# Turns and first scores of three attentions issued inside the projection panels ahead of them

## The reference, cut to what matters

```
(a_q, a_k, a_v, a_g, b_cq, b_ckv, b_kr, b_g, c_q, c_k, c_v, c_g) = split(h @ w_in)
o_a = dense attention, 8 query heads on 2 key heads, normalised and rotated q and k, times silu(a_g)
cq = rms_norm(b_cq);  q_nope, q_pe = split(cq @ w_uq);  q_pe is rotated
ckv = rms_norm(b_ckv); k_nope, vb = split(ckv @ w_ukv); k_pe = rotated b_kr
o_b = dense attention on [nope, pe], 4 heads, times silu(b_g)
o_c = neighbourhood attention with a bias table, 4 heads, times silu(c_g)
x + rms_norm(concat(o_a, o_b, o_c) @ w_out)
```

## Time and profile before

| what | us |
|---|---|
| median of 3 runs | 3577.71 (3576.12 to 3578.48) |
| the profiled execution's own time | 3576.41 |
| its span | 3574.4 |
| TensorE matmul busy | 3421.8 (96%) |
| VectorE busy | 1803.3 (50%) |
| ScalarE busy | 1099.3 (31%) |

### The profile page before, as it was taken

One profiled execution on the slowest core, in us unless ns is written; L12 is line 12 of the kernel. 1 busy time (PEld: TensorE's weight loads), 2 busy tenths in 40 slices (PEclk: granted clock), 3 DMA queues, 4 the chain that ended last, 5 costly groups with the idle time before them and its releaser, 6 DMA issues.

```text
span 3574.4 us, 49995 instructions
## 1 busy us (share of the span) xinstructions
PE 3421.8 (96%) x17285; PEld 2755.7 (77%) x17285; DVE 1803.3 (50%) x3264; ACT 1099.3 (31%) x1764; POOL 151.8 (4%) x218
## 2 busy tenths in 40 slices
PE   7999999999999999999997999999997999999997
PEld 6878878668788788786885888778786888778786
DVE  4555665544565557753456332625634332535643
ACT  3232243232232322522323222523323322433321
POOL 1101001000111010010010000000000000000000
PEclk9999999999999999999998999999998999999999
DMA  7636414215676363060364333033233333123242
GB/s 263 209 91 195 133 42 162 77 42 200 179 257 188 102 188 89 18 215 12 122 190 146 99 95 99 19 92 104 107 129 110 89 94 99 43 86 92 79 155 97
DMA packets 183840, 429.83 MB, mean 120 GB/s; under 512 B 18166, under 2 KB 25777, under 8 KB 177240
## 3 DMA queue, kind: packets, MB, share of 16 engines
q1 hardware_dynamic: 151144, 297.65, 26.1%
q0 software_dynamic: 28992, 104.43, 9.6%
q10 hardware_dynamic: 3504, 25.22, 1.8%
HBM read 406.15 MB, written 24.75 MB: 121 GB/s over the span
## 4 chain that ended last, share of the span: by engine, by line
PE 60%; DVE 4%; issue 1%; DMA 1%; ACT 1%; DVEq 0%; SPq 0%; ACTq 0%; POOLq 0%
PE bank L660 16%; PE bank L662 16%; PE bank L661 16%; PE bank L705 2%; PE bank L723 2%; PE bank L860 1%; PE bank L838 1%; PE bank L849 1%; PE bank L697 1%; PE bank L714 1%; PE bank L684 1%; DMA stage<-in_w_out 1%; PE bank L893 0%; DMA wmod<-in_w_mod 0%; PE bank L930 0%
## 5 line engine op out<-in xcount | busy, mean ns | idle before, releaser
L660 PE MATMUL bank<-wlo,act_hi 128*128 128x512 f32 (+1 forms) x3968 | 1552.3, 391 | 7.9 <-DVE zone L1483 4.6
L662 PE MATMUL bank<-whi,act_lo 128*128 128x512 f32 (+1 forms) x3968 | 1539.1, 388 | 0.0
L661 PE MATMUL bank<-whi,act_hi 128*128 128x512 f32 (+1 forms) x3968 | 1538.2, 388 | 0.0
L1436 DVE TENSOR_TENSOR wlo<-stage,whi 128x1024 fp32r<-128x1024 f32 (+1 forms) x496 | 598.3, 1210 | 794.1 <-ACT whi L1089 792.3
L1089 ACT ACTIVATE whi<-stage 128x1024 fp32r<-128x1024 f32 (+1 forms) x496 | 514.9, 1048 | 1458.0 <-PE bank L662 796.2
L660 PEld LDWEIGHTS bank<-wlo,act_hi 128*128 128x128 f32 x3968 | 747.1, 188 | 178.4 <-issue 21.2
L662 PEld LDWEIGHTS bank<-whi,act_lo 128*128 128x128 f32 x3968 | 746.4, 188 | 151.8
L661 PEld LDWEIGHTS bank<-whi,act_hi 128*128 128x128 f32 x3968 | 747.2, 188 | 145.9
L1451 DVE SCALAR_TENSOR_TENSOR macc<-wmod,csil,macc 128x512 f32<-128x512 f32 x360 | 270.0, 750 | 111.4 <-DMA wmod<-in_w_mod 82.3
L2275 POOL DMA_DIRECT2D wmod<-in_w_mod x192 | 136.6, 711 | 1736.9 <-DVE macc L1451 1720.9
L723 PE MATMUL bank<-zone 128*128 128x128 f32 x1024 | 134.7, 276 | 0.0
(11 more groups left out here) (236 smaller groups left out, 2308.3 us busy)
## 6 DMA issues: line engine op xcount, KB each, us to landing
stage<-in_w_in SPq DMA_DIRECT2D x352, 512.0 KB, 3.8
wmod<-in_w_mod POOLq DMA_DIRECT2D x192, 512.0 KB, 4.5
stage<-in_w_out SPq DMA_DIRECT2D x128, 512.0 KB, 4.1
out<-Y ACTq DMA_DIRECT2D x20, 1024.0 KB, 5.5
zone<-out SPq DMA_DIRECT2D x4, 4096.0 KB, 14.9
stage<-in_w_in SPq DMA_DIRECT2D x16, 320.0 KB, 3.8
Y<-in_x ACTq DMA_DIRECT2D x4, 1024.0 KB, 9.3
rpb_tiles<-rpb_pad POOLq DMA_DIRECT2D x16, 224.0 KB, 7.2
```

Of the source, the lines that this page charges most:

```text
L660: pe.matmul(out, hi_x, lo_w, start=(k == 0), stop=False)
L661: pe.matmul(out, hi_x, hi_w, start=False, stop=False)
L662: mm = pe.matmul(out, lo_x, hi_w, start=False, stop=(k == KC - 1))
L1436: dve.tensor_tensor(wlo[:, j % RH, :, 0:width], stage[:, j % RS, :, 0:width], whi[:, j % RH, :, 0:width].bitcast(F32), ALU.subtract).then_ ...
```

## The change

1. C: its 8 turn jobs are issued in panel 3, two after each of j = 0 to 3, into banks 4 and 5 (`job_bank`); after j = 6 its first two scores. VectorE takes the jobs at its own j = 2 to 5, takes the first two row maxima ahead of the gate, and ScalarE the first two exponentials ahead of the tanh. The tanh goes to another place (`tanh_c`).
2. A: in panel 8, after j = 4 the two key turns, after j = 5 the first query turn, after j = 6 two scores. The turn of head h + 1 moves from the first to the last unit of head h, into banks 2 and 3, and the next unit waits for its copy.
3. B: the turns of three cq chunks go behind j = 6 of panel 11 into banks 4 to 6 and are copied out by ScalarE after the tanh. The four v products alternate with the four q_pe turns, and head h waits for its own turn only.
4. P: in panel 6, the turns of 2 key and 2 query tiles after j = 0 to 3, two scores after j = 6. The later turns move to the last unit of a group of four, two groups ahead. Banks are dealt anew. The wait for all finishes at the end goes into panel 7, at its first use of banks 1 and 3.
5. `banks_free` before C, A and P goes; the units 2 and 3 wait for single banks, since turned probabilities now go to banks 0 and 1 (for P, bank 0).

The diff of TensorE's side, and of the others the lines that are spoken of (P's and C's parts on ScalarE and VectorE follow the same form):

```diff
-        PAIR_SCORE, PAIR_TURN, PAIR_OUT, PAIR_JOB = [bank[2:4], bank[4:6]], bank[6], [bank[7], bank[1]], bank[0]
+        PAIR_SCORE, PAIR_TURN, PAIR_OUT, PAIR_JOB = [bank[4:6], bank[6:8]], bank[0], [bank[1], bank[3]], bank[2]
         MSUM = bank[7]
         SIDE = bank[4:6]
+        EARLY = bank[4:7]
+        A_JOB = bank[2:4]
...
+        A_EARLY, P_EARLY, BEGUN = A_KV + 1, 4, 2
+        def job_bank(n):
+            if 1 <= n < 1 + 2 * C_H + A_EARLY:
+                return SIDE[n % 2]
+            if 1 <= n < 1 + 2 * C_H + A_KV + A_H:
+                return A_JOB[n % 2]
+            return JOB[n % 2]
...
-            def attention(blk, l, br, early=None):
+            def attention(blk, l, br, turned=None, more=None, opened=None):
                 n = 4 * br["heads"]
-                for i in range(n + 3):
-                    if early and i % 4 == 0 and i < n:
-                        early(i // 4)
+                for i in range(br["begun"], n + 3):
+                    if turned and i % 4 == 0 and i < n:
+                        turned(i // 4)
                     if i < n:
                         score(blk, l, br, i)
+                    if opened:
+                        opened(i)
+                    if more and i % 4 == 3 and i < n:
+                        more(i // 4)
...
-                with pe.Fori(1, 4) as p:
+                with pe.Fori(1, 3) as p:
                     panel(0, l, p, row=p - 1)
-                banks_free(l, 4)
-                pe.wait_ge(mod_ev.sem, mod_ev.at(0, l, 3))
-                for n, jb in enumerate(JOBS_C):
-                    job(0, l, BR_C["j0"] + n, jb)
-                pe.wait_ge(job_ev.sem, job_ev.at(0, l, BR_C["j0"] + 8))
-                attention(0, l, BR_C)
+                j0 = BR_C["j0"]
+                def begin_c(j):
+                    if j < 4:
+                        job(0, l, j0 + 2 * j, JOBS_C[2 * j])
+                        job(0, l, j0 + 2 * j + 1, JOBS_C[2 * j + 1])
+                    if j == 6:
+                        pe.wait_ge(job_ev.sem, job_ev.at(0, l, j0 + 8))
+                        apart(pe)
+                        for i in range(BEGUN):
+                            score(0, l, BR_C, i)
+                panel(0, l, 3, row=2, between=begin_c)
+                def opened_c(i):
+                    if i in (2, 3):
+                        pe.wait_ge(lin_free[i - 2].sem, lin_free[i - 2].at(0, l, 4))
+                    if i == 3:
+                        pe.wait_ge(mod_ev.sem, mod_ev.at(0, l, 3))
+                attention(0, l, BR_C, opened=opened_c)
...
-                panel(0, l, 8)
-                banks_free(l, 9)
-                pe.wait_ge(mod_ev.sem, mod_ev.at(0, l, 7))
-                pe.wait_ge(prep.sem, prep.at(0, l, A_READY + 1))
-                j0 = BR_A["j0"]
-                for n, jb in enumerate(JOBS_AK + JOBS_AQ[0:1]):
-                    job(0, l, j0 + n, jb)
-                def next_queries(h):
+                i0 = BR_A["j0"]
+                def begin_a(j):
+                    if j == 4:
+                        pe.wait_ge(prep.sem, prep.at(0, l, A_READY + 1))
+                        apart(pe)
+                        job(0, l, i0, JOBS_AK[0])
+                        job(0, l, i0 + 1, JOBS_AK[1])
+                    if j == 5:
+                        job(0, l, i0 + 2, JOBS_AQ[0])
+                    if j == 6:
+                        pe.wait_ge(job_ev.sem, job_ev.at(0, l, i0 + 3))
+                        apart(pe)
+                        for i in range(BEGUN):
+                            score(0, l, BR_A, i)
+                panel(0, l, 8, between=begin_a)
+                def opened_a(i):
+                    if i in (2, 3):
+                        pe.wait_ge(lin_free[i - 2].sem, lin_free[i - 2].at(0, l, 9))
+                    if i == 3:
+                        pe.wait_ge(mod_ev.sem, mod_ev.at(0, l, 7))
+                        for t in (2, 3):
+                            pe.wait_ge(lin_free[t].sem, lin_free[t].at(0, l, 9))
+                        apart(pe)
+                def turned_a(h):
+                    pe.wait_ge(job_ev.sem, job_ev.at(0, l, i0 + 3 + h))
+                    apart(pe)
+                def more_a(h):
                     if h + 1 < A_H:
-                        job(0, l, j0 + 3 + h, JOBS_AQ[h + 1])
-                    pe.wait_ge(job_ev.sem, job_ev.at(0, l, j0 + 3 + h))
-                attention(0, l, BR_A, next_queries)
+                        job(0, l, i0 + 3 + h, JOBS_AQ[h + 1])
+                attention(0, l, BR_A, turned_a, more_a, opened_a)
...
+                def begin_b(j):
+                    if j == 6:
+                        pe.wait_ge(prep.sem, prep.at(0, l, BTM_READY + 1))
+                        for r in range(3):
+                            apart(pe)
+                            for t in range(TT):
+                                mm = pe.transpose(EARLY[r][:, tok(t)], cq_b[:, t, tok(r)], ident[:, :])
+                            mm.then_inc(cq_turned.sem, 1)
+                panel(0, l, 11, row=8, between=begin_b)
...
+                pe.wait_ge(cq_out.sem, cq_out.at(0, l, 3))
+                apart(pe)
+                for jb in JOBS_B2[0:TT + 2 * B_H]:
                     job(0, l, n, jb)
                     n += 1
                 pe.wait_ge(prep.sem, prep.at(0, l, QPE_READY + 1))
-                for jb in JOBS_B3:
-                    job(0, l, n, jb)
-                    n += 1
-                pe.wait_ge(job_ev.sem, job_ev.at(0, l, n))
-                attention(0, l, BR_B)
+                apart(pe)
+                for h in range(B_H):
+                    job(0, l, n, JOBS_B2[TT + 2 * B_H + h])
+                    job(0, l, n + 1, JOBS_B3[h])
+                    n += 2
+                def turned_b(h):
+                    pe.wait_ge(job_ev.sem, job_ev.at(0, l, B_VQ + 2 * h + 2))
+                    apart(pe)
+                def opened_b(i):
+                    if i == 2:
+                        pe.wait_ge(job_ev.sem, job_ev.at(0, l, n))
+                        apart(pe)
+                attention(0, l, BR_B, turned_b, None, opened_b)
...
-                for n in range(J_KT, J_QT + 1):
-                    pair_job(l, n)
-                for i in range(PAIRS + 3):
+                for i in range(BEGUN, PAIRS + 3):
+                    hp = i // 4
                     if i % 4 == 0 and i < PAIRS:
-                        hp = i // 4
-                        if hp + 1 < S_H // 2:
-                            pair_job(l, J_QT + hp + 1)
                         pe.wait_ge(job_ev.sem, job_ev.at(1, l, J_QT + hp + 1))
+                        apart(pe)
                     if i < PAIRS:
                         pair_score(l, i)
+                    if i < 4:
+                        for t in ((0,), (1, 2, 3))[i - 2]:
+                            pe.wait_ge(lin_free[t].sem, lin_free[t].at(1, l, 7))
+                        apart(pe)
+                    if i % 4 == 3 and hp + 2 < S_H // 2:
+                        pair_job(l, J_QT + hp + 2)
                     if 2 <= i < PAIRS + 2:
                         pair_turn(l, i - 2)
                     if i >= 3:
                         pair_pv(l, i - 3)
-                pe.wait_ge(fin_done.sem, fin_done.at(1, l, PAIRS))
...
+                def begin_p(j):
+                    if j == 0:
+                        pe.wait_ge(prep.sem, prep.at(1, l, S_READY + 1))
+                        apart(pe)
+                    if j < P_EARLY:
+                        pair_job(l, J_KT + j)
+                    if j == 6:
+                        pe.wait_ge(job_ev.sem, job_ev.at(1, l, J_KT + P_EARLY))
+                        apart(pe)
+                        for i in range(BEGUN):
+                            pair_score(l, i)
+                panel(1, l, 6, between=begin_p)
                 swa(l)
                 apart(pe)
-                panel(1, l, 7, between=lambda j: rank_sums(l, j))
+                def last_pairs(t):
+                    if t in (1, 3):
+                        pe.wait_ge(fin_done.sem, fin_done.at(1, l, PAIRS - (t == 1)))
+                panel(1, l, 7, between=lambda j: rank_sums(l, j), opened=last_pairs)
...
                 if after:
                     for j in range(LEAD):
                         split_hi(blk, l, p + 1, j, next_width)
+                if begin:
+                    begin()
                 if row is not None:
                     mod_row_out(l, row)
                 if take:
...
-                in_panel(l, 3, take_tanh(), row=2)
+                in_panel(l, 3, take_tanh(tmp=tanh_c), row=2, begin=begun(BR_C, l))
...
+                act.wait_ge(lin_done.sem, lin_done.at(0, l, 12 * TT))
+                for r in range(3):
+                    act.wait_ge(cq_turned.sem, cq_turned.at(0, l, r + 1))
+                    act.activation(cqT[:, r, :], EARLY[r][:, :], ACT.Copy, scale=cols[:, B_QC + r:B_QC + r + 1])\
+                       .then_inc(cq_out.sem, 1)
```

(33 more changed lines are left out.)

132 lines of the change are left out of this document (72 added, 60 removed).

## The result

The changed kernel takes 3524.25 us (median of 4 runs, 3522.68 to 3526.52) against 3577.22 for the kernel before, run beside it; the ratio is 0.9849, 95% interval 0.9837 to 0.9862. That is 53.0 us less; a gain of 53.5 and a time of 3524.2 were forecast. The page's busy line answers to the earlier trace rows: TensorE lost 24 us of busy time (matmuls at the low clock count as longer) and the other 27 us are idle time.

A forecast was written before the change was run, and what follows sets the result against it. TensorE, with a matmul in flight for 96% of the span, was taken to bound the kernel; 13.0 + 10.5 + 3.9 + 3.2 + 2.8 + 17.9 + 2.2 = 53.5 us saved, 3577.7 - 53.5 = 3524.2, range 3512 to 3545.

The forecast's parts named there:

- C: Attention start at panel 3: 5.35 us inside plus 1.63 behind, 6.98 against 13.51; 13.0 us saved in two layers.
- A: Attention start at panel 8: 2.74 us inside, 5.8 in all against 11.55 and 10.54; 10.5 us saved.
- B: Attention start at panel 11: savings of 3.9 us at the start, 3.2 at values and q_pe turns, 2.8 for clock.
- P: Attention start at panel 6: 3.3 us inside, 3.6 behind, 17.9 saved; wait of 1.10 at the end hidden, 2.2 saved.
- B's clock: First score to unit 3's in B: full clock could give 5.5 us in both layers or nothing; half taken, 2.8.
- B's other two terms: Last panel matmul to first product in B, 3.9 us saved; values and q_pe turns, 1.6 a layer, 3.2 saved.
- score 2's price: Third score of C, behind the panel: 0.96 us with the change of operand type, 0.86 without.
- rival 2: Panels become bound by VectorE, `split_lo` and weight DMAs come late: 68 us lost against 53.5, 3592 us; chance 0.04.
- the head turns: Other six heads of A: each turn's copy takes about 1.45 us against 1.33 of cover; 0.12 each, 0.7 a layer.
- 1 (low clock comes back): Low clock returns at A, B and P, and A's head turns cost 0.5 each: gain 37, 3541 us; chance 0.19.
- Rival 3: Low clock vanishes everywhere and A's turns find their copy done: gain 59, 3519 us; chance 0.12.
- 4: First scores wait for their turns' copies after j = 6, so panels' idle only moves: gain some 20, 3558; chance 0.03.

The follow-up runs named there:

- late_c: The changed kernel with C's turns and first two scores behind panel 3 again, after all four gates: 3539.59 us.
- b_old: The changed kernel with B's cq turns behind panel 11 and v products ahead of the q_pe turns again; third bank, ScalarE copies, own-turn wait kept: 3523.47 us.
- late_p2: The changed kernel with P's four turns and first two scores behind panel 6 of the second block again: 3546.97 us.
- a_turn: The changed kernel with A's turn job of head h + 1 issued at the third unit of head h, save for the first head: 3522.75 us.

## Why the prediction was right, and where it was not

The time was forecast to 0.1 us (the gain to 0.5, as the kernel before ran 0.5 us faster beside it), but by misses that cancel, and that is luck: from the 53.5 of the sum, 2.4 more in B's clock, 1.1 in P, 0.35 in C and 1.7 elsewhere, against 6.3 at panels 10 and 11, 1.2 in A and 0.2 in B's other two terms, make the 51.3 of the two spans.

- **C** held step by step: 5.31 inside where 5.35 was forecast, 1.52 behind for 1.63. The 0.11 is what score 2's price held for a change of operand type: directly behind the panel's matmuls the first score takes 0.85 (212.98 to 213.83), so the 0.96 of the earlier trace rows came with the wait of 0.95 that stood ahead of that score, and not with the type. That the panel grows by just what is put in shows that VectorE never bound it; rival 2's place (`wlo` waits) stayed empty. late_c confirms the size (14.6, 1.0 of it clock).
- **A.** Inside 2.37 and 2.29 for 2.74. The failed term is the head turns: 0.29 each instead of 0.12. The score comes 1.96 us behind the start of the job, so 1.52 behind its end where I had 1.45 for the copy, against 1.33 of cover; and I had left out the 0.10 that TensorE loses as it starts again. The forecast's 2.63 to 2.8 between two scores with a head's turn job between them was 2.83 to 2.93.
- **B.** Both sizes were right and both reasons wrong. I gave the 1.6 a layer at the values to the alternation; b_old shows that the wait for one head instead of four earns it. The prediction's own working could have told: "three waits of 0.44 and one of 1.41 for three of 0.6" makes 0.9 and not 1.6, and by starts, less 0.44 for the turn, the waits of before are 0.60, 0.63 and 0.63, the same as in b_old, and 1.60 at the end. I gave the start to turns inside the panel; b_old does without them and keeps the gain, which leaves the third bank and ScalarE. Only a kernel that undoes one of several edits of a place could show this. The clock term came in full, 5.2 for the 5.5 it could be, where I took half; it went with the idle 1.41 ahead of the first score, with which the clock fell in 7 of 8 passes.
- **P.** 3.60 and 3.77 behind the panel for 3.6, 2.94 and 2.98 inside for 3.3, 1.30 for 1.10 at the end. late_p2 puts 19.8 us on the start, low clock included.
- **The failed step** is the sentence "No part of the chain outside these places changes: no DMA is added or moved". None is, in the program; but TensorE's code itself comes by DMA, and 405 instructions more ahead of panel 10 put one of its fetches into a stretch that is bound by transfers: 6.3 us lost at panels 10 and 11, of which 6.0 came back with the fetch moved. I had looked at how long the panels are and what waits in them, not at what the DMA queues of kind "instruction" do.
- **Rivals.** 1 (low clock comes back) held in half of B's starts, for 2 us each, not at A and P. In the profile of after that was no loss against before, whose clock fell there too. Rival 3's clock came, but not its other condition, that A's turns find their copy done. The Trainium skill's page "TensorE: Matmul & The Clock Gate", Part 1, says that the count of matmuls at the low clock varies from run to run. The trace agrees: at B's start in the first layer the four microseconds from 4 us behind the panel are at 0.54 in after and at 1.00 in a_turn, and TensorE's program there is the same. 4 had no part: no score inside a panel waits.

## What to carry to other kernels

Where an attention begins behind a projection, put its turns and first scores between the panel's matmuls: they cost what they cost elsewhere, and the wait for the gate, the copies and the first exponential goes, and with it the clock that those waits lose. After such an edit compare every stretch, also those that it does not touch: the count of instructions ahead of a transfer-bound stretch is a parameter of it, and a panel taken out of a loop changes it by some 400. And when several edits meet in one place, undo them one by one before one of them gets the credit.

## What the runs showed of the hardware

- With a fetch of code on a DMA queue (0.02 MB in 0.96 us) 9.7 to 10.7 us into panel 10, a 512 KB transfer comes 1.3 us later. From panel 10's first matmul to panel 11's last, B's turns taken off, it is 76.2 to 78.3 us in the 12 passes with no delay and 78.6 to 81.5 in the 14 with it. About half of the difference is low clock: with half of the time at 0.50 taken off (an estimate from the granted clocks), the two groups are 75.9 to 76.6 and 76.9 to 78.3.
- 96 semaphore increments among a panel's matmuls cost TensorE nothing that shows (43.42 to 43.41 us).
- The same code at B's start falls to a clock of 0.53 in one layer and not in the next; the stretch costs 1.7 to 2.4 us more then.
- Behind the panels of C, A and P the clock stayed at 1.00 in 54 of 54 passes with the starts in the panel, and fell in 21 of 30 with them behind it.
- A score behind a wait takes 0.96 us and directly behind other matmuls 0.85, so TensorE loses 0.10 as it starts again.
